# The down projection of the prompt rows as seven products of quarters

## The reference, cut to what matters

```python
act = jax.nn.gelu(c[..., :D_FF], approximate=True) * c[..., D_FF:]   # (rows, 2816)
x = x + rmsnorm(act @ ffn_w_down, g_ffn_post)                        # ffn_w_down: (2816, 1024)
```

## Time and profile before

| what | us |
|---|---|
| median of 3 runs (1565.37 to 1569.6) | 1567.13 |
| the profiled execution | 1567.42 |
| its span | 1565.7 |
| TensorE busy, of the span | 1524.1 (97%) |
| VectorE busy | 898.4 (57%) |
| ScalarE busy | 583.8 (37%) |
| GpSimd busy | 300.0 (19%) |

### The profile page before, as it was taken

How to read it: one execution, slowest core, us unless ns; L and a number is a source line. 1 busy time by engine, 2 the same in 40 slices (tenths; PEclk the granted TensorE clock), 3 DMA queues, 4 the chain that set the end, 5 groups by cost and what they waited for, 6 DMA issues and landing times.

```text
span 1565.7 us, 26850 instructions
## 1 busy us (share of the span) xinstructions
PE 1524.1 (97%) x10067; PEld 1415.8 (90%) x10067; DVE 898.4 (57%) x1545; ACT 583.8 (37%) x1084; POOL 300.0 (19%) x293
## 2 busy tenths in 40 slices
PE   7999999999999999999997999999999999999997
PEld 7889999989999999997877999999999998788875
DVE  6575465657332233226558777777777775554644
ACT  7233132333222122114445444444444444453432
POOL 1124133340100000000124333333333320000000
PEclk9999999999999899999998999999999999999999
DMA  7234455451332432304114666655662138665471
GB/s 259 59 109 132 142 174 173 141 173 35 112 113 69 121 110 67 121 14 135 71 45 125 218 218 199 219 191 188 220 221 83 64 111 300 226 216 177 157 243 66
DMA packets 145809, 227.65 MB, mean 145 GB/s; under 512 B 14011, under 2 KB 116441, under 8 KB 144831
## 3 DMA queue, kind: packets, MB, share of 16 engines
q1 hardware_dynamic: 136711, 203.97, 40.8%
q0 software_dynamic: 8736, 22.08, 3.8%
q10 hardware_dynamic: 288, 0.59, 0.1%
HBM read 196.46 MB, written 74.34 MB: 173 GB/s over the span
## 4 chain that ended last, share of the span: by engine, by line
PE 91%; DVE 4%; DMA 2%; ACT 1%; issue 1%; SPq 0%; ACTq 0%; DVEq 0%
PE PS L1323 28%; PE PS L1144 19%; PE PS L1389 13%; PE PS L1039 9%; PE PS L1282 6%; PE PS L1020 4%; PE PS L1208 2%; PE PS L1096 2%; PE PS L1068 1%; PE PS L1384 1%; PE PS L1082 1%; PE PS L1252 1%; PE PS L1001 1%; DMA as_stage<-acts 1%; PE PS L1052 1%
## 5 line engine op out<-in xcount | busy, mean ns | idle before, releaser
L1323 PE MATMUL PS<-h_lo,wr_hi 128*128 128x264 f32 x1056 | 216.7, 286 | 0.0
L1323 PEld LDWEIGHTS PS<-h_lo,wr_hi 128*128 128x128 f32 x1056 | 165.6, 190 | 0.0
L1323 PE MATMUL PS<-t_hi,wr_hi 128*128 128x264 f32 x704 | 149.9, 292 | 7.6 <-DVE h_lo L2296 4.1
L2334 DVE TENSOR_TENSOR wd_lo<-wd_stage,wd_hi 128x1024 fp32r<-128x1024 f32 x66 | 80.8, 1224 | 118.3 <-ACT as_hi L1762 118.2
L1323 PE MATMUL PS<-h_hi,wr_hi 128*128 128x264 f32 x704 | 145.5, 288 | 0.7 <-DVE cext L2362 0.5
L1323 PE MATMUL PS<-t_hi,wr_lo 128*128 128x264 f32 x704 | 145.3, 286 | 0.0
L2020 DVE TENSOR_TENSOR tw_lo<-tw_stage,tw_hi 128x1024 fp32r<-128x1024 f32 (+1 forms) x28 | 32.6, 1166 | 177.7 <-ACT tw_hi L1533 177.5
L1323 PEld LDWEIGHTS PS<-t_hi,wr_hi 128*128 128x128 f32 x704 | 110.8, 191 | 9.1 <-DVE h_lo L2296 4.7
L1761 ACT ACTIVATE wd_hi<-wd_stage 128x1024 fp32r<-128x1024 f32 x66 | 69.8, 1057 | 130.9 <-PE PS L1389 76.6
L1144 PE MATMUL PS<-hT_hi,tw_hi 128*128 128x352 f32 x480 | 111.2, 342 | 1.8 <-issue 1.8
L1323 PEld LDWEIGHTS PS<-h_hi,wr_hi 128*128 128x128 f32 x704 | 108.9, 189 | 3.5 <-DVE wr_lo L2286 0.7
(11 more groups left out here) (317 smaller groups left out, 3444.3 us busy)
## 6 DMA issues: line engine op xcount, KB each, us to landing
wd_stage<-in_ffn_w_down SPq DMA_DIRECT2D x66, 512.0 KB, 3.6
tw_stage<-in_ffn_w_up SPq DMA_DIRECT2D x88, 256.0 KB, 4.8
out_k_s<-in_cache_k_w SPq DMA_DIRECT2D x8, 2044.0 KB
out_v_s<-in_cache_v_w SPq DMA_DIRECT2D x8, 2044.0 KB
qb<-zs SPq DMA_DIRECT2D x24, 512.0 KB, 5.1
acts<-cact POOLq DMA_DIRECT2D x22, 528.0 KB, 9.4
tw_stage<-in_w_in SPq DMA_DIRECT2D x20, 512.0 KB, 5.3
as_stage<-acts SPq DMA_DIRECT2D x44, 192.0 KB, 3.9
```

The lines of the kernel that those rows point to most:

```text
L1323: last = pe.matmul(PS[:, bank + b, 0:BH], w[slot][:, k, :], x[:, k, b * BH:(b + 1) * BH], start=(k == 0 and j == 0), stop=(k == HK - 1 and ...
L2334: dve.tensor_tensor(wd_lo[slot][:, :], wd_stage[slot][:, :], wd_hi[slot][:, :].bitcast(F32), ALU.subtract)
```

## The change

The 1024 prompt rows are cut into two halves of 512 rows, the 2816 channels into two halves of 11 blocks (HK2), the 1024 columns into two halves of 512. The four quarter products per result quarter (eight in all) become seven (`PRODUCTS`, in the order 1, 2, 6, 7, 4, 5, 3), of sums and differences of quarters. A slot `(n, k)` is block k of product n: 4 tiles x 3 passes of 512 columns. Samples are multiplied as before; their low columns ride on the slots of products 1 and 2, their high columns in 11 slots `(0, k)` between those of products 6 and 7.

- All weights stay in SBUF (`dw`), loaded once in products 1 and 2, and so do the activations of one quarter (`dS`). Activations of the others are loaded again for each product, into four stages (`ds`).
- GpSimd makes the sums of weights (T1, T4a, T2, T3, T4b) and the sums of rows S1, Sa and Sb, each 128x512, in the written order; VectorE makes the sums of rows for products 6 and 7 (`row_sum`), two slots ahead of their use.
- ScalarE splits (`split_down`), now 512 and 512 wide; it may be three slots ahead of TensorE (`ring`), and further for the last four of product 3 (LATE = 4).
- Results of a product are added into C1 and C2 in SBUF by VectorE (`evict`, at the second slot of the next product; two additions for product 5), the first product's copied by ScalarE. Six PSUM banks go round (`bank_free`).
- Finished tiles in SBUF: ScalarE squares, VectorE or, for finished tiles 1 to 3, GpSimd scales them by the gain (`scale_rows`), VectorE multiplies and adds the residual row, which SyncE loads tile by tile (`load_row`). Five of the nine are finished while product 3 runs or after it from earlier products; the four of product 3 come last.
- Where the up projection ends, three slots are prepared in place of four blocks, and VectorE's loop goes on when the last `cnat` is made.

```diff
--- before.py
+++ after.py
@@ -292,13 +292,11 @@
...
+            dw_lo.append(a(f"dw_lo{3 + e}", [P, 512], F32R))
+            da_hi.append(b(f"da_hi{3 + e}", [P, 512], F32R))
+            da_lo.append(b(f"da_lo{3 + e}", [P, 512], F32R))
+        HK2, LATE = FC // 2, 4
+        PRODUCTS = (1, 2, 6, 7, 4, 5, 3)
+        SLOTS = []
+        for n in PRODUCTS:
+            for k in range(HK2):
+                SLOTS.append((n, k))
+                if n == 6 and k % 2 and k < 10:
+                    SLOTS.append((0, k // 2))
+                if n == 7 and k % 2 == 0:
+                    SLOTS.append((0, 5 + k // 2))
...
+        SUMS = [("T1", k) for k in range(HK2)] + [(c, k) for k in range(HK2) for c in ("S1", "T4a")]
+        SUMS += [("T2", k) for k in range(HK2)] + [("T3", k) for k in range(HK2)]
+        SUMS += [("T4b", k) for k in range(HK2)] + [("Sa", k) for k in range(HK2)] + [("Sb", k) for k in range(HK2)]
...
+        def operands(x):
...
+            return {0: (dw[k][:, high], dw[HK2 + k][:, high]) if n == 0 else None,
+                    1: (dw[k][:, low], st[:, 0, :]) if n == 1 else None,
+                    2: (dw[HK2 + k][:, low], st[:, 0, :]) if n == 2 else None,
+                    3: (dw[HK2 + k][:, high], dS[:, k, :]),
+                    4: (dw[HK2 + k][:, low], st[:, 0, :]) if n == 4 else None,
+                    5: (dw[k][:, low], dS[:, k, :]),
+                    6: (st[:, 1, :], st[:, 0, :]) if n == 6 else None,
+                    7: (st[:, 1, :], st[:, 0, :]) if n == 7 else None}[n]
+
...
+            def load_down(x):
+                n, k = x
+                u = STAGE[x]
+                st, signal = ds[u % 4], wd_in[u % 4]
+                if u >= 4:
+                    m, l = STAGED[u - 4]
+                    sp.wait_ge(wd_lo_done, AT[STAGED[u - 4]] + 1)
+                    if m in (2, 3, 5):
+                        sp.wait_ge(d_sum, summed_at({2: "S1", 3: "Sb", 5: "Sa"}[m], l))
+                f = k + (HK2 if n in (2, 4, 3) else 0)
+                if n == 2:
                     sp.wait_ge(act_out[f % 2], 16 * (f // 2 + 1))
...
+                if n in (1, 2):
+                    sp.dma_start(dw[f][:, :], w_dn[f]).then_inc(signal, 16)
+                if n in (2, 7):
+                    sp.dma_start(st[:, :, :], acts[f * P:f * P + P, 0:TP].rearrange("p (b t) -> p b t", b=2)).then_inc(signal, 16)
+                else:
+                    half = TP // 2 if n == 4 else 0
+                    sp.dma_start(st[:, 0, :], acts[f * P:f * P + P, half:half + TP // 2]).then_inc(signal, 16)
...
+            load_down((1, 0))
+            load_smp(0)
...
+            sp.wait_ge(p_done, 7 * FC - 2 + U0)
+            load_down((1, 1))
             sp.wait_ge(p_done, 7 * FC - 1 + U0)
-            load_down(3)
+            load_down((1, 2))
+            load_down((1, 3))
             sp.wait_ge(p_done, 7 * FC + U0)
+            load_down((1, 4))
+            load_s(0)
+            load_down((1, 5))
+            sp.wait_ge(cnat_out, 32 * FC)
+            load_down((1, 6))
+            load_s(1)
+            load_down((1, 7))
+            sp.wait_ge(c_out, 7 * FC + U0)
+            load_s(2)
+            for i in range(2):
+                sp.wait_ge(act_out[i], 16 * (FC // 2))
+            load_smp(1)
+            load_down((1, 8))
             sp.dma_start(gfin[:, :], io["norm_ffn_post"][0].partition_broadcast(P)).then_inc(gain_in, 16)
 
+            def load_row(i):
+                n = FINAL[i]
+                t0, rows = tile_of(n)
+                if i >= 2:
+                    sp.wait_ge(y_ready, i - 1)
+                else:
+                    sp.wait_ge(wd_lo_done, AT[5, 1 + i] + 1)
+                sp.dma_start(xrow[i % 2][0:rows, :], x2s[t0:t0 + rows, :]).then_inc(wq_in[1][i % 2], 16)
...
+            for x in STAGED[9:]:
+                load_down(x)
+                if x == (3, 5):
+                    load_row(0)
+                    load_row(1)
+            for i in range(NTILE):
+                store_y(i)
+                if i + 2 < NTILE:
+                    load_row(i + 2)
...
+            for k in range(HK2):
+                pool.wait_ge(wd_lo_done, AT[1, k] + 1)
+                down_sum("T1", k, dw[k][:, low], dw[k][:, high], dw[k][:, low], ALU.subtract)
+            for k in range(HK2):
+                st = staged(2, k)
+                pool.wait_ge(x_in[k // 4], 16 * (4 if k < 4 else 3))
+                down_sum("S1", k, dS[:, k, :], dS[:, k, :], st[:, 1, :], ALU.add)
+                pool.wait_ge(wd_lo_done, AT[2, k] + 1)
+                down_sum("T4a", k, dw[HK2 + k][:, low], dw[HK2 + k][:, low], dw[k][:, low], ALU.add)
+            for k in range(HK2):
+                st = staged(6, k)
+                down_sum("T2", k, st[:, 1, :], dw[HK2 + k][:, high], dw[k][:, low], ALU.subtract)
+            for k in range(HK2):
+                st = staged(7, k)
+                pool.wait_ge(t_lo_done, rows_at(7, k))
+                down_sum("T3", k, st[:, 1, :], dw[HK2 + k][:, high], dw[k][:, high], ALU.subtract)
+            for k in range(HK2):
+                down_sum("T4b", k, dw[HK2 + k][:, low], dw[HK2 + k][:, high], dw[HK2 + k][:, low], ALU.subtract)
+            for k in range(HK2):
+                st = staged(5, k)
+                pool.wait_ge(wd_lo_done, AT[5, k] + 1)
+                down_sum("Sa", k, dS[:, k, :], dS[:, k, :], st[:, 0, :], ALU.subtract)
+
+            def scale_rows(i):
+
+                rows = finished(FINAL[i])
+                pool.wait_ge(o_ss, 9 + i + 1)
+                pool.tensor_tensor(rows, rows, in_halves(gfin[:, :]), ALU.mult).then_inc(t_sums, 1)
+            for k in range(HK2):
+                st = staged(3, k)
+                down_sum("Sb", k, dS[:, k, :], st[:, 0, :], dS[:, k, :], ALU.subtract)
+                if k == 6:
+                    pool.wait_ge(gain_in, 64)
+                    scale_rows(1)
+                elif k == 8:
+                    scale_rows(2)
+            scale_rows(3)
...
-                        if f == 0 and n == 0:
+
+            def tile_part(x, i):
+                n, k = x
+                r, bank = ring(x), (4 * PRODUCTS.index(n) + i) % 6
+                for j, (a, w) in enumerate(((da_hi, dw_hi), (da_hi, dw_lo), (da_lo, dw_hi))):
...
+            for x in SLOTS[:-LATE]:
+                n, k = x
+                r = ring(x)
+                pe.wait_ge(wd_lo_done, AT[x] + 1)
...
+                for i in (2, 3, 0, 1) if n == 1 else range(4):
+                    if k == 0:
+                        if n == 1 and i == 0:
                             pe.wait_ge(c_out, 7 * FC + U0)
...
+                        bank_free(n, i)
+                    mm = tile_part(x, i)
+                    if k == HK2 - 1 and i < 3 and n != 1:
+                        mm.then_inc(f_mm, 1)
...
+                mm.then_inc(wd_used, 1)
+                if n == 1 and k == 2:
+                    turn_tails(FC - 1)
+            for i in range(4):
+                for x in SLOTS[-LATE:]:
+                    pe.wait_ge(wd_lo_done, AT[x] + 1)
+                    mm = tile_part(x, i)
+                    if i == 3:
+                        mm.then_inc(wd_used, 1)
+                if i < 3:
+                    mm.then_inc(f_mm, 1)
...
+            def split_down(x):
+                n, k = x
+                r = ring(x)
+                if n in (1, 2, 4):
+                    act.wait_ge(wd_in[STAGE[x] % 4], stage_in[x])
+                for c in {4: ("T4b",), 5: ("S1", "T1"), 7: ("T3",), 6: ("T2",), 3: ("Sb",)}.get(n, ()):
+                    act.wait_ge(d_sum, summed_at(c, k))
+                if n in (6, 7):
+                    act.wait_ge(t_lo_done, rows_at(n, k))
...
+                if r >= 3:
+                    act.wait_ge(wd_lo_done, AT[5, HK2 - 1] + 1)
+                elif AT[x] >= 3:
+                    act.wait_ge(wd_used, AT[x] - 2)
+                w, a = operands(x)
+                act.activation(dw_hi[r][:, :], w, ACT.Copy)
+                act.activation(da_hi[r][:, :], a, ACT.Copy).then_inc(wd_hi_done, 1)
...
-            split_down(2)
+            split_down(SLOTS[2])
             tails(FC - 1)
-            split_down(3)
             gelu(FC - 1)
             tails_out(FC - 1)
...
+            for s_, x in enumerate(SLOTS[3:], 3):
+                split_down(x)
...
+                if x == (2, 1):
+                    act.wait_ge(act_out[1], 16 * (FC // 2))
+                    act.wait_ge(wd_used, AT[1, HK2 - 1] + 1)
+                    for i in range(4):
+                        act.activation(C1[:, i, 512:D], PS[:, i, :], ACT.Copy).then_inc(u_out, 1)
+                if x[0] == 3 and 3 <= x[1] < 8:
+                    square(x[1] - 3)
+            for i in range(5, NTILE):
+                square(i)
...
-                                             as_hi[slot][:, whole:wide].bitcast(F32), ALU.subtract)
-                last.then_inc(wd_lo_done, 1)
+            def low_down(x):
```

(73 more changed lines are left out.)

314 lines of the change are left out of this document (155 added, 159 removed).

## The result

The changed kernel takes 1596.57 us (median, 1595.5 to 1600.22) against 1567.4 for the kernel before: 1.019 times as long, 95% interval 1.0168 to 1.0212. Its profiled execution has a span of 1593.9 us, 28.2 more than before. The direction was forecast, the size was not: 9.6 us slower was the forecast, 29 came, 4.6 us above the range.

What follows compares the result with a forecast made beforehand. TensorE was taken to bound the down projection by its count of matmuls; 31.1 us of gain against 40.7 us of added waits made it 9.6 us slower, 1576.7 us, range 1551 to 1592.

Steps and rivals of the forecast that it cites:

- c: Products 2, 6 and 7: VectorE and GpSimd take turns on SBUF operands; TensorE waits 12 us (2 to 25).
- a: Hand-over from the up projection: three prepared slots run out before VectorE is ready; wait 3.5 us (2.5 to 4.5).
- b: Product 1's transfers: block 6 issued late, later blocks share one queue with other loads; wait 3.5 us (1 to 7).
- f: End of product 3: last subtractions stand behind multiply-adds waiting for GpSimd's scalings; wait 13 us (3.3 to 15).
- d: Turn from product 7 to 4: evictions stand behind a subtraction; wait 1.5 us (0.8 to 3.5).
- e: Turn from product 5 to 3: GpSimd's first sum queued late, evictions follow; wait 3.2 us (1.6 to 6).
- h: Last tiles: an added addition out of PSUM and VectorE slower per tile than TensorE; 1 us (0 to 1.5).
- g: Lower granted clock while TensorE is partly idle at the end of product 3; 3 us (0 to 6).
- Rival 1: VectorE and GpSimd don't hinder each other; waits 15.0 us, 16.1 us faster, 1551; chance 0.22.
- Rival 2: The engines hinder each other, but product 3's scalings fall in gaps; waits 31.7 us, 1568, no change; chance 0.18.
- Rival 3: Transfers bound products 1 and 2; 12 us more than forecast, 1588; chance 0.12.
- Wrong: Listed counter-signs: GpSimd sums of 1.3 us beside busy VectorE, last product without holes, transfer waits in products 1 and 2.

## Why the prediction was right and wrong

The gain side held: 924 + 88 matmuls, 0.227 us apart where nothing is late, and none of the kernels has a product shorter than its count.

**The sum.** By the table the waits came to 59.0 us where the prediction added up 40.7. Against their terms c measured 10.0 us more, a and b 5.1, f 3.9, d 1.4, e and h 0.9; g's 3 us have no row of their own, since the products hold them, and 21.3 less 3 is the difference.

**c is the step that failed.** Products 2, 6 and 7 lost 4.9, 5.0 and 12.1 us, 22.0 against 12. The bound of 25 was low by its own working: with holds of 1.29 and 0.69 the three products come to 26 us over, before the turns between them. The mechanism was read rightly from the earlier trace rows, and the price of a pair too (0.58 + 1.17 = 1.75 forecast, 1.70 measured). What failed is the sentence "Their sum per product": it counts each GpSimd sum in the product that needs it. The sums for product 4 wait only for each other, so their queue runs them as soon as those for product 7 are through, beside VectorE's fullest stretch: ten subtractions from 1456.59 on last 1.75 to 1.78 us each instead of 0.69. Product 4 was put at 26 against 30 us, and had the room; pacing took 4.8 us off product 7 and 1.0 off product 4. That is about half of what c had wrong. With pacing product 7 still loses 7.3 us; 3.04 of them are one hole at the turn from product 6, put at 1.75, and some 3 are matmuls at the lower clock behind its holes. Without GpSimd's arithmetic the three products lose 2.2 us, about the low bound of 2 that was given.

**a** came as forecast in its mechanism; its size depends on the execution. In the profiled one the hole is 5.34 us instead of 3.5 (bound 4.5). The chain of waits goes back to a transfer that landed after 5.71 us: it made TensorE late, ScalarE stood 1.65 us for TensorE before it could split the slot, and so the two subtractions that TensorE waited for met four of GpSimd's first sums (answers the earlier trace rows; the last VectorE step of the gate, two subtractions, ScalarE's wait, GpSimd's burst):

```profile
1309.18 0.18 DVE L2600 TENSOR_TENSOR cact<-cgel,cacc 128x32 f32<-128x32 f32 x1
1311.17 2.07 DVE L2528 TENSOR_TENSOR dw_lo<-dw,dw_hi 128x512 fp32r<-128x512 f32 x1 [1.80 <-ACT da_hi L1944]
1313.17 1.74 DVE L2529 TENSOR_TENSOR da_lo<-ds,da_hi 128x512 fp32r<-128x512 f32 x1
...
1309.66 0.37 ACT L1977 ACTIVATE cnat<-PS 18x256 f32<-18x256 f32 x1 [1.65 <-PE PS L1460]
...
1311.40 6.33 POOL L1088 TENSOR_TENSOR dw<-dw 128x512 f32<-128x512 f32 x4
```

In five kernels above with the same product 1 (row sums on GpSimd, finishing moved, fillers, evictions earlier, sums paced) the two subtractions run ahead of GpSimd's sums, and the hole is 2.90 us in each, within the bounds, as it is without GpSimd's arithmetic. The first row below is the hole of the kernel with earlier evictions, the second one that b gave there:

```profile
1308.96 0.50 PE L1534 MATMUL PS<-dw_hi,da_hi 128*128 128x512 f32 x1 [2.90 <-DVE da_lo L2529]
...
1326.24 0.60 PE L1534 MATMUL PS<-dw_hi,da_hi 128*128 128x512 f32 x1 [2.63 <-DVE da_lo L2529]
```

Put at nothing in the prediction was a wait in product 1's first slot, where the third tile needs a PSUM bank that VectorE still reads for the convolution: 2.02 us in the profiled execution, 0.6 to 1.0 in the five.

**b** had its mechanism right, with block 6 issued only behind the last convolution state (SyncE's issues, answers the earlier trace rows):

```profile
1298.91 0.45 SPq L874 DMA_DIRECT2D ds<-acts  x1
1313.01 0.33 SPq L869 DMA_DIRECT2D dw<-in_ffn_w_down  x1
```

Between the two SyncE stands for 14 us. In the profiled execution, where TensorE was late already, no hole shows behind it; in the five it is one of 1.4 to 2.8 us (3.5 forecast, 1 to 7), behind the transfer of the second sample part that stands in the same queue, and moving the loads took 6.0 us off product 1 in the kernel without the turns. Product 1 lost 12.1 us in the profiled execution and some 9.3 to 10.7 in the five, against 7 for a and b; the rest is the first slot's wait and the lower clock, which had been booked under g.

**d and e** were 2.9 against 1.5 in product 4 (within its bounds, with the end of the burst in it), and 1.3 in product 5 plus 2.2 in the first slot of product 3 against 3.2: the second size as forecast.

**f** gave single slots, subtractions behind multiply-adds and lengthened turns, as written. Product 3 lost 19.1 us, of which 2.2 belong to e: 16.9, where 13 were forecast, bound 15. The missing share is not blocking alone: with GpSimd left out product 3 still lost 10.6, where "below 3.3, without blocking" stood. The low bound was wrong, since it left out that VectorE's multiply-add waits for residual rows. Rows of product 3 show a subtraction and the scaling beside it in the changed kernel, and then, with GpSimd left out, a multiply-add that waits 4.92 us for its row, behind which TensorE stood for 4.90:

```profile
1556.51 2.81 DVE L2529 TENSOR_TENSOR da_lo<-dS,da_hi 128x512 fp32r<-128x512 f32 x1
...
1554.86 3.93 POOL L1120 TENSOR_TENSOR C<-C,gfin 128x1024 f32<-128x1024 f32 x1
```

```profile
1534.21 1.28 DVE L2703 SCALAR_TENSOR_TENSOR C<-C,prstd,xrow 128x1024 f32<-128x1024 f32 x1 [4.92 <-DMA xrow<-x2s]
```

**g** should not have been a term of its own. By TensorE's timeline some 15 us of matmul time were lost at the lower level (starts 0.33 to 0.43 apart instead of 0.227), five times the 3 forecast, and filling the holes brought the clock back and the time down by 1 us for product 3, and by 0.1 for product 1 of the kernel without GpSimd's arithmetic. A reading that fits both is that the low clock stands behind waits for another engine or a transfer, where a slow matmul only shortens the next wait; for products 6 and 7 it was not tried. **h** was 1.6 against 1.

**The rivals.** Rival 1 fell as a forecast (1.70 us a pair), and its own time was wrong too: with the turns gone by two different edits the kernel takes 1564 to 1565, not 1551, for the waits of product 1 and of the residual rows. Rival 2 fell with c and f. Rival 3's mechanism, transfers as the pace of product 1, is there, at some 6 us, and reaches the end only in a kernel without the turns; product 2, which it named as well, takes its 35.1 us as soon as GpSimd is quiet. What "Wrong" listed was a good list, and it missed a case: all signs right and one queue run ahead.

By the Trainium skill's rule (SBUF — State Buffer, Who interferes with whom) the pairs of c and f contend, and the trace agrees (1.70 us a pair). What two instructions do when they meet was read rightly; when they meet was a matter of GpSimd's queue, and that was the error.

## What to carry to other kernels

Where two engines take turns, don't count an instruction in the stage that needs it but where its own queue lets it start; a producer with nothing to wait for runs in a burst, and one wait that holds it back to the stretch with room was worth 5.9 us in the two products concerned (7.9 between the medians). Give sums with both operands in SBUF to one engine when both are busy: 1.70 us for a pair against 1.2 for two on VectorE (15.2 us for this kernel, where the sums were moved nearer to their use as well), and put the loads that TensorE wants next ahead of those it wants a product later (6.0 us of product 1). Waits of the bound engine add up only while it is the bound; read the chain of each stage first, and fill a hole for a test before a low clock behind it gets a price of its own. Look for a hole in a second execution before it is explained: the 5.34 us of the hand-over were 2.90 in five kernels with the same code there.

## What the hardware showed that I had not expected

- The turns are one for one over long stretches: in the rows of product 2 above, and in the burst from 1456.59 on, each subtraction alternates with exactly one sum, though alone one starts every 0.60 and 1.25 us; neither engine gets two in a row there.
- What a subtraction loses goes by GpSimd's instruction: 0.42 us beside a copy of 512 columns, 1.10 beside a sum of 512, 2.2 beside a scaling of 1024 (one every 2.8 against 0.60); beside memsets of 0.53 us nothing.
- The granted clock came back to 1.0 (0.93 in the last stretch) when holes of 1.1 to 4.0 us were filled with matmuls on a spare bank, and that was worth 1.0 and 0.1 us.
